# Inverting the gated delta rule's triangular matrices with block transposes on VectorE

## The chip, the cores and the metric

The kernel runs on one core of one Trainium2 chip. The metric is the device time of one execution in microseconds (us). Three executions of the kernel before took 2325.54, 2326.91 and 2327.57 us; their median, 2326.91 us, is the time before.

The engines are named as in the profile: PE (TensorE matmul), PEld (its weight loads), DVE (VectorE), ACT (ScalarE), POOL (GpSimd), SP (SyncE, which issues the weight DMAs).

## The reference, cut to what matters

Two layers, each with four token mixers and an MLP over 512 tokens of width 1024. The change concerns one mixer, the gated delta rule (4 heads, key and value width 128, chunks of 64 tokens):

```
h = rmsnorm(x, n_pre_mix); proj = h @ w_in
qkv = silu(causal_dwconv(gdn_qkv, conv_w))
beta = sigmoid(gdn_b); g = -exp(a_log) * softplus(gdn_a + dt_bias)
gc = cumsum(g over the chunk)                      # 8 chunks of 64 tokens
decay = exp(gc[c] - gc[s]) for c >= s
lower = strict lower part of (k * beta) @ k.T * decay       # 64 x 64 for each chunk and head
t_inv = inverse of (eye + lower)                   # triangular_solve
u = t_inv @ (v * beta); w = t_inv @ (k * beta * exp(gc))
attn = q @ k.T * decay
# over the chunks: v_new = u - w @ state; o = q*exp(gc) @ state + attn @ v_new
#                  state = state * exp(g_last) + k_dec.T @ v_new
```

The other parts (windowed attention, stick-breaking attention, retention, the output projections and the MLP) are as they were in both kernels.

## The kernel before, in words

All weights are float32. POOL splits every weight tile that SP loads into a high and a low part (lines 581 and 583), and a product of activations and weights is three fp32r matmuls (high by high, low by high, high by low) of 512 columns: line 1722, in `unit`. A unit is 256 rows of a weight matrix for 512 outputs: four output tiles by two row tiles by three matmuls. POOL may convert a further unit when PE has begun the next one (semaphore `w_used`).

The delta rule works on blocks of 128 tokens (two of the reference's chunks), numbered 0 to 3, with one 128 x 256 tile for the four heads' matrices: partition rows 0 to 63 and 64 to 127 hold two 64 x 64 matrices of each head. Blocks are inverted in pairs (b0 = 0, then b0 = 2), so there are two inverses in each layer and four in an execution. The two blocks of a pair, e = 0 and 1, are interleaved to cover each other's latencies.

The inverse is built by doubling. `g_T[e]` holds the running inverse in one orientation and `g_V[e]` its transpose; they are block diagonal. Level 0 is done on DVE (`first_level` writes `g_V`). Then, in the loop `for b0 in (0, 2)` of `tensor_layer`:

- T0: 64 x 64 matmuls with the identity turn `g_V` into `g_T`, by way of PSUM and an ACT copy (line 803).
- For level n = 1 to 5: Y = masked lower matrix times the even halves of T (PE), ACT copies Y out of PSUM (line 808), X = V times Y (PE), DVE subtracts X from the even halves of T (line 1409), V = T turned by matmuls with the identity (PE), ACT copies the turned halves to `g_V` (line 815), or at level 5 to `g_U` (line 818). A level n merges diagonal blocks of 2^n into blocks of 2^(n+1): after level 4 they are 32 wide, after level 5 64 wide.
- Level 6 joins the two chunks of a block (Y and X only).

`level_mask` on DVE (line 1245) makes the masked matrix of level n + 1 while level n runs. Between Y and X of levels 2, 3, 5 and 6 PE computes a quarter of a gate unit: one output tile with both row tiles, six matmuls (`QUARTERS`). In the trace all mixer matmuls have line 1867 (`MM1`), and one program matmul there counts as two instructions, so a Y or X or V pass over both blocks (16 matmuls) reads x32.

On DVE, `row_decays` (lines 1377 to 1380: a copy and two products) of the pair's blocks follow the X subtractions of levels 2 and 3. On ACT, the four value silus (`conv_silu(8)` to `(11)`, line 727) stand before the T0 copies. After the first inverse, blocks 0 and 1 run the recurrence, and prepare blocks 2 and 3 on the way. Block 3's score matmuls (`scores_gdn(3)`) and their masking on DVE (`scores_out(3)`, lines 1369 and 1371) come at the very end of that, ahead of the second inverse.

All orders are written out by hand: each engine runs its own program in order, and they meet at semaphores. `mixer_keys` lists the PSUM tiles of the mixers in order; they take four banks in turn, and a tile waits until the one four places before it has been freed.

## Time and profile before

| | us |
|---|---|
| median of three executions (lowest, highest) | 2326.91 (2325.54, 2327.57) |
| profiled execution, first to last instruction (span) | 2324.0 |
| PE busy in it | 2297.4 (99%) |
| DVE, ACT, POOL busy | 851.0, 751.4, 1282.2 |
| first inverse, from its T0 to the transposes behind it | 25.3 |

The span is the profiled execution's own time between its first and its last instruction; the median lies 2.9 us above it, which is what lies around the instructions. The granted TensorE clock was 0.997 over the span and 1.00 in the inverses, so 2.4 GHz. A busy PE in these rows is one with a matmul in flight: starts that lie further apart than the work needs do not show as idle time. So the places of the change are read from start to start.

### The profile page before, as it was taken

Reading aid. Unit: us, or ns where it says so; the run is one execution under the profiler, and the core shown is the slowest. Engines: PE = TensorE matmul, PEld = TensorE weight load, DVE = VectorE, ACT = ScalarE, POOL = GpSimd, SP = SyncE. Lnnn points to the kernel's source line nnn. Section 1 sums busy time; section 2 is a strip of 40 time slices with the busy share of each in tenths; the row PEclk is TensorE's granted clock in tenths of the full one; section 3 lists DMA queues with packets and bytes.
Section 4 is the critical chain, followed back from the end, with each engine's and each line's share of the span. In section 5 each row is a group of like instructions: output and inputs, shape, how many; then the busy total and the mean of one; then the engine's idle time right before and its main releaser. Section 6 shows DMA issues by size and latency. Waiting matters only on the chain.

```text
span 2324.0 us, 31844 instructions
## 1 busy us (share of the span) xinstructions
PE 2297.4 (99%) x13054; PEld 1870.2 (80%) x13054; DVE 851.0 (37%) x1350; ACT 751.4 (32%) x1505; POOL 1282.2 (55%) x732
## 2 busy tenths in 40 slices
PE   8999999999999999999999999999999999999998
PEld 7788877877877888888887888778778778888887
DVE  4543225334445521123355430254243445112233
ACT  5633226213035321122355341451230544112121
POOL 5513654554554566677655136546555445666874
PEclk9999999999999999999999999999999999999999
DMA  4311331322221243322222113213222213333331
GB/s 151 91 38 47 95 87 46 118 82 86 75 89 52 92 124 92 100 94 97 82 79 85 36 54 93 73 60 115 84 88 84 74 60 101 108 100 94 97 100 64
DMA packets 105904, 196.72 MB, mean 85 GB/s; under 512 B 8480, under 2 KB 18848, under 8 KB 105504
## 3 DMA queue, kind: packets, MB, share of 16 engines
q1 hardware_dynamic: 104608, 188.40, 26.8%
q10 hardware_dynamic: 1152, 6.29, 0.8%
q8 instruction: 104, 1.70, 0.3%
q14 instruction: 40, 0.33, 0.0%
HBM read 192.57 MB, written 2.10 MB: 84 GB/s over the span
## 4 chain that ended last, share of the span: by engine, by line
PE 96%; ACT 2%; DVE 2%; issue 1%; DMA 0%; DVEq 0%; ACTq 0%
PE big L1722 71%; PE mix L1722 9%; PE mix L1867 5%; PE big L2074 1%; PE mix L2042 1%; PE mix L2144 1%; PE mix L2053 1%; PE mix L1827 1%; PE mix L2272 0%; PE mix L2225 0%; PE mix L1781 0%; ACT o_hi L618 0%; PE mix L2209 0%; PE mix L2195 0%; PE mix L1999 0%
## 5 line engine op out<-in xcount | busy, mean ns | idle before, releaser
L583 POOL TENSOR_TENSOR ring_lo<-stage,ring_hi 128x1024 fp32r<-128x1024 f32 (+3 forms) x364 | 912.4, 2507 | 30.4
L581 POOL TENSOR_SCALAR ring_hi<-stage 128x1024 fp32r<-128x1024 f32 (+3 forms) x364 | 371.3, 1020 | 987.9 <-PE big L1722 906.6
L1722 PE MATMUL big<-h_hi,ring_hi 128*128 128x512 f32 (+1 forms) x1888 | 720.6, 382 | 3.0 <-DVE h_lo L1173 1.8
L1722 PE MATMUL big<-h_hi,ring_lo 128*128 128x512 f32 (+1 forms) x1888 | 709.3, 376 | 0.0
L1722 PE MATMUL big<-h_lo,ring_hi 128*128 128x512 f32 (+1 forms) x1888 | 709.2, 376 | 0.0
L1722 PEld LDWEIGHTS big<-h_hi,ring_hi 128*128 128x128 f32 x1888 | 355.4, 188 | 75.1 <-issue 8.6
L1722 PEld LDWEIGHTS big<-h_lo,ring_hi 128*128 128x128 f32 x1888 | 355.4, 188 | 65.7
L1722 PEld LDWEIGHTS big<-h_hi,ring_lo 128*128 128x128 f32 x1888 | 355.7, 188 | 62.9 <-issue 1.4
L1663 DVE TENSOR_TENSOR h_lo<-scr,h_hi 128x1024 fp32r<-128x1024 f32 x64 | 84.7, 1323 | 248.5 <-ACT h_hi L1091 248.5
L1722 PE MATMUL big<-ring_hi,h_hi 128*128 128x512 f32 x448 | 174.2, 390 | 0.0
L1722 PE MATMUL big<-ring_lo,h_hi 128*128 128x512 f32 x448 | 174.1, 390 | 0.0
L1722 PE MATMUL big<-ring_hi,h_lo 128*128 128x512 f32 x448 | 173.7, 389 | 0.0
L1091 ACT ACTIVATE h_hi<-scr 128x1024 fp32r<-128x1024 f32 x64 | 68.5, 1070 | 262.2 <-PE big L1722 260.2
L1674 DVE SCALAR_TENSOR_TENSOR scr<-big,scr 128x512 f32<-128x512 f32 x64 | 44.3, 692 | 254.5 <-ACT scr L1100 254.3
L1722 PE MATMUL mix<-ring_hi,h_hi 128*128 128x512 f32 x320 | 125.0, 391 | 0.0
L1722 PE MATMUL mix<-ring_hi,h_lo 128*128 128x512 f32 x320 | 124.6, 389 | 0.0
L1722 PE MATMUL mix<-ring_lo,h_hi 128*128 128x512 f32 x320 | 124.5, 389 | 0.0
L1100 ACT ACTIVATE scr<-big 128x512 f32<-128x512 f32 x64 | 38.3, 598 | 262.1 <-PE big L1722 261.3
L1722 PEld LDWEIGHTS big<-ring_hi,h_hi 128*128 128x128 f32 x448 | 84.1, 188 | 18.4 <-issue 0.7
L1722 PEld LDWEIGHTS big<-ring_hi,h_lo 128*128 128x128 f32 x448 | 84.1, 188 | 17.7
L1722 PEld LDWEIGHTS big<-ring_lo,h_hi 128*128 128x128 f32 x448 | 83.8, 188 | 18.0 <-POOL ring_lo L583 1.0
L1722 PE MATMUL big<-o_hi,ring_hi 128*128 128x512 f32 x224 | 90.2, 403 | 1.0 <-ACT scr L676 0.9
(304 smaller groups left out, 2758.0 us busy)
## 6 DMA issues: line engine op xcount, KB each, us to landing
stage<-in_w_in SPq DMA_DIRECT2D x168, 512.0 KB, 3.5
stage<-in_w_mlp_in SPq DMA_DIRECT2D x64, 512.0 KB, 3.7
stage<-in_w_mlp_out SPq DMA_DIRECT2D x64, 512.0 KB, 3.6
stage<-in_w_o SPq DMA_DIRECT2D x16, 512.0 KB, 3.6
stage<-in_w_br_a SPq DMA_DIRECT2D x8, 512.0 KB, 3.6
stage<-in_w_br_c SPq DMA_DIRECT2D x8, 512.0 KB, 3.6
stage<-in_w_br_d SPq DMA_DIRECT2D x8, 512.0 KB, 3.6
stage<-in_w_br_b SPq DMA_DIRECT2D x8, 512.0 KB, 3.6
```

What stands on the lines that cost most here:

```text
L581: nc.gpsimd.tensor_scalar(rH[jw][0:pp, r, 0:kk, 0:job.n], w, 1.0, 0.0, ALU.mult, ALU.add).then_inc(sem("w_hi"), 1)
L583: nc.gpsimd.tensor_tensor(rL[jw][0:pp, r, 0:kk, 0:job.n], w, f32(rH[jw][0:pp, r, 0:kk, 0:job.n]), ALU.subtract).then_inc(sem("w_ready"), 1)
L1091: A(hH[:, q:q + 2, :], fT[:, 2 * u:2 * u + 2, :], ACT.Copy).then_inc(sem("f_hi"), 1)
L1100: A(fT[:, 4 * g + i, :], ps[:, :], ACT.Relu).then_inc(sem("f_relu"), 1)
L1663: TT(hL[:, q:q + 2, :], fT[:, 2 * u:2 * u + 2, :], f32(hH[:, q:q + 2, :]), ALU.subtract).then_inc(sem("f_lo"), 1)
L1674: big_free(STT(fT[:, k, :], ps[:, :], 0.0, fT[:, k, :], ALU.max, ALU.mult), (f"up{g}", i))
L1722: ins_ = MM(o_, a_, r_, start=s0, stop=s1)
L1827: done(MM(ps[:, :], f32(ones_r[:, 0:1]).to_broadcast((P, P)), q_sq[:, i % 4, :], start=True, stop=True), ("l2", i))
L1867: return MM(o_, a_, b_, start=True, stop=True)
L2042: i = MM(c_bank[u][:, at:at + w], hv(cK, h)[:, j * P:(j + 1) * P], hv(cQ, h)[:, j * P:], start=opens, stop=True, skip_group_check=True)
L2053: MM(c_bank[u][:, :], rot_r[:, 2 * P:3 * P], part[:, u, :], start=False, stop=True, skip_group_check=True)
L2074: r = MM(c_out[e * DH:e * DH + DH, j * P:], cV[:, j, (2 * p + e) * DH:(2 * p + e + 1) * DH], c_A[:, u, at:at + S - j * P], start=j == 0, s ...
```

## The change

What it does:

- T0 and the V passes of levels 1 to 4 leave PE and ACT. As all diagonal blocks are at most 32 wide there, DVE's transpose, which turns every 32 x 32 block of a tile by itself, gives the same result: `first_inverse(b)` turns `g_V` into `g_T`, `inverse_turned(b, n)` turns `g_T` into `g_V`, each one instruction over 128 x 256 float32. The V pass of level 5 (blocks of 64) stays on PE and ACT.
- The gate unit that PE works on within an inverse is dealt in eighths (one output tile, one row tile: three matmuls) instead of quarters: after Y of all six levels and after X of levels 1 and 4.
- `row_decays` of the pair follow the levels 4 and 5 instead of 2 and 3. `natural_k_v(0)` waits for block 1's, as its output shares memory with what they read.
- The silus of value tiles 10 and 11 come after ACT's Y copies of levels 1 and 2 instead of before T0.
- `scores_gdn(3)` moves up on PE to stand behind `lower(3)`, ahead of `new(1)`. On DVE `scores_out(3)` is split: the product with the decays comes before `first_level(3)`, the masking (which overwrites what `o(1)` reads) waits for `o(1)`.
- The PSUM tiles of the mixers fall by 20 a layer, a multiple of the four banks, so the tiles behind keep their banks.

```diff
-QUARTERS = (2, 3, 5, 6)
+EIGHTHS = (("Y", 1), ("X", 1), ("Y", 2), ("Y", 3), ("Y", 4), ("X", 4), ("Y", 5), ("Y", 6))
...
     for b0 in (0, 2):
-        k += [("T0", b0), ("T0", b0 + 1)]
         for n in range(1, LEVELS):
-            for t in "YXV" if n < LEVELS - 1 else "YX":
+            for t in "YXV" if n == LEVELS - 2 else "YX":
                 k += [(t, b0 + e, n) for e in range(2)]
...
             k += [("R", b + 2), ("B", b + 2), ("LT", b + 2)] if ahead else []
+            k += [("att", 3)] if b == 1 else []
             k += [("new", b), ("o", b), ("dS", b)]
-        if b0 == 0:
-            k.append(("att", 3))
...
-            for i in range(8, 12):
-                conv_silu(i)
+            conv_silu(8)
+            conv_silu(9)
             for b0 in (0, 2):
-                for e in range(2):
-                    ps = mix_wait(act, ("T0", b0 + e))
-                    act.wait_ge(*upto("a_attd", b0 + e + 1))
-                    mix_free(A(g_T[e], ps[:, 0:GH * HB], ACT.Copy), ("T0", b0 + e))
...
+                    if b0 == 0 and n in (1, 2):
+                        conv_silu(9 + n)
-                    for e in range(2) if n < LEVELS - 1 else ():
+                    for e in range(2) if n == LEVELS - 2 else ():
                         ps = mix_wait(act, ("V", b0 + e, n))
...
+            def first_inverse(b):
+                dve.wait_ge(*upto("a_attd", b + 1))
+                mix_freed(dve, ("LT", b))
+                V.transpose(g_T[b % 2], g_V[b % 2]).then_inc(sem("a_T0"), 1)
+            def inverse_turned(b, n):
+                mix_freed(dve, ("X", b, n))
+                V.transpose(g_V[b % 2], g_T[b % 2]).then_inc(sem("a_V"), 1)
...
                         mix_free(i, key)
-                    if n in (2, 3):
-                        row_decays(b0 + n - 2)
+                    for e in range(2) if n < LEVELS - 2 else ():
+                        inverse_turned(b0 + e, n)
+                    if n in (4, 5):
+                        row_decays(b0 + n - 4)
...
                         lower(b + 2)
+                        if b == 1:
+                            scores_out(3)
                         first_level(b + 2)
+                        if b == 1:
+                            first_inverse(3)
+                    if b == 1:
+                        scores_masked(3)
                     ps = mix_wait(dve, ("dS", b))
...
+            def eighth(t, n):
+                if (t, n) in EIGHTHS:
+                    i = EIGHTHS.index((t, n))
+                    unit(*(fills.pop(0) if i == 7 else fills[0]), (i // 2,), rows_of=range(i % 2, i % 2 + 1))
...
-                        mix_freed(pe, ("T0", b0 + e) if n == 1 else ("X", b0 + e, n - 1))
+                        if n == 1:
+                            pe.wait_ge(*upto("a_T0", b0 + e + 1))
+                        else:
+                            mix_freed(pe, ("X", b0 + e, n - 1))
...
-                        if n > 1:
+                        if n == LEVELS - 1:
                             mix_freed(pe, ("V", b0 + e, n - 1))
+                        elif n > 1:
+                            pe.wait_ge(*upto("a_V", (LEVELS - 3) * b0 + 2 * (n - 2) + e + 1))
...
+                    if b == 1:
+                        scores_gdn(3)
                     mix_freed(pe, ("ks", b))
                     mix_freed(pe, ("X", b, LEVELS - 1))
```

PE's row in the first inverse, before: T0, then Y, X and V of level 1, Y of level 2, a quarter of the gate unit, and X of level 2. `big` is a gate's bank, `mix` a mixer's, `g_uc` is `g_V`, `consts` the identity, `scr` all else of the mixer.

```order
L1867 MATMUL mix<-consts,g_uc 64x64 x16
L1867 MATMUL mix<-scr 64x32 x16
L1867 MATMUL mix<-scr,g_uc 64x32 x16
L1867 MATMUL mix<-consts,scr 64x32 x16
L1867 MATMUL mix<-scr 64x32 x16
L1722 MATMUL big<-h_hi,ring_hi 128x512
L1722 MATMUL big<-h_hi,ring_lo 128x512
L1722 MATMUL big<-h_lo,ring_hi 128x512
L1722 MATMUL big<-h_hi,ring_hi 128x512
L1722 MATMUL big<-h_hi,ring_lo 128x512
L1722 MATMUL big<-h_lo,ring_hi 128x512
L1867 MATMUL mix<-scr,g_uc 64x32 x16
```

The change, from the same place: Y of level 1, an eighth, X, an eighth, Y of level 2, an eighth.

```order
L1895 MATMUL mix<-scr 64x32 x16
L1744 MATMUL big<-h_hi,ring_hi 128x512
L1744 MATMUL big<-h_hi,ring_lo 128x512
L1744 MATMUL big<-h_lo,ring_hi 128x512
L1895 MATMUL mix<-scr,g_uc 64x32 x16
L1744 MATMUL big<-h_hi,ring_hi 128x512
L1744 MATMUL big<-h_hi,ring_lo 128x512
L1744 MATMUL big<-h_lo,ring_hi 128x512
L1895 MATMUL mix<-scr 64x32 x16
L1744 MATMUL big<-h_hi,ring_hi 128x512
L1744 MATMUL big<-h_hi,ring_lo 128x512
L1744 MATMUL big<-h_lo,ring_hi 128x512
```

The two passes with `consts` are gone, and every run of `big` rows is three long.

DVE's row over levels 1 to 3 before: masks (line 1245), subtractions of X (line 1409), the first row decays (1377 to 1380).

```order
L1245 TENSOR_TENSOR scr<-scr,consts 128x256 x2
L1409 TENSOR_TENSOR scr<-scr,mix 128x64x2 x2
L1245 TENSOR_TENSOR scr<-scr,consts 128x256 x2
L1409 TENSOR_TENSOR scr<-scr,mix 128x32x4 x2
L1377 COPY st<-scr 128x4
L1379 TENSOR_TENSOR scr<-scr 128x4x128
L1380 TENSOR_TENSOR scr<-scr 128x512
L1245 TENSOR_TENSOR scr<-scr,consts 128x256 x2
L1409 TENSOR_TENSOR scr<-scr,mix 128x16x8 x2
```

The change, levels 1 to 3: masks (now line 1238), subtractions (now line 1424), and the transposes of both blocks (line 1368).

```order
L1238 TENSOR_TENSOR scr<-scr,consts 128x256 x2
L1424 TENSOR_TENSOR scr<-scr,mix 128x64x2 x2
L1368 STREAM_TRANSPOSE g_uc<-scr 128x256 x2
L1238 TENSOR_TENSOR scr<-scr,consts 128x256 x2
L1424 TENSOR_TENSOR scr<-scr,mix 128x32x4 x2
L1368 STREAM_TRANSPOSE g_uc<-scr 128x256 x2
L1238 TENSOR_TENSOR scr<-scr,consts 128x256 x2
L1424 TENSOR_TENSOR scr<-scr,mix 128x16x8 x2
L1368 STREAM_TRANSPOSE g_uc<-scr 128x256 x2
```

Two transposes stand behind each pair of subtractions, so the masks of the level after next stand behind the transposes; the row decays have left these levels.

DVE's row at the end of block 1 before: `scores_out(2)`, `lower(3)`, `first_level(3)`, the four state updates of block 1 (line 1433).

```order
L1369 TENSOR_TENSOR mix<-mix,scr 128x512
L1371 TENSOR_TENSOR scr<-mix,consts 128x512
L1349 TENSOR_TENSOR mix<-mix,scr 128x256
L1351 TENSOR_TENSOR scr<-mix,scr 64x256
L1353 TENSOR_TENSOR scr<-mix,consts 128x256
L1360 TENSOR_TENSOR mix<-mix,consts 128x256
L1364 TENSOR_TENSOR g_uc<-scr,mix 128x256
L1433 SCALAR_TENSOR_TENSOR scr<-scr,st,mix 128x128 x4
```

The change: `lower(3)`, the first half of `scores_out(3)` (line 1373), `first_level(3)`, `first_inverse(3)` (1363), the masking of block 3's scores (1383), the state updates (1457), and the first masks of the second inverse.

```order
L1342 TENSOR_TENSOR mix<-mix,scr 128x256
L1344 TENSOR_TENSOR scr<-mix,scr 64x256
L1346 TENSOR_TENSOR scr<-mix,consts 128x256
L1373 TENSOR_TENSOR mix<-mix,scr 128x512
L1353 TENSOR_TENSOR mix<-mix,consts 128x256
L1357 TENSOR_TENSOR g_uc<-scr,mix 128x256
L1363 STREAM_TRANSPOSE scr<-g_uc 128x256
L1383 TENSOR_TENSOR scr<-mix,consts 128x512
L1457 SCALAR_TENSOR_TENSOR scr<-scr,st,mix 128x128 x4
L1238 TENSOR_TENSOR scr<-scr,consts 128x256 x2
```

Block 3's masking now stands ahead of block 1's state updates, with a wait for PE's `o(1)`.

## Rows read from the trace of the kernel before

**Rows 1.** The page, parts 1 and 4: engines; share of the span by line.

```profile
PE 2297.4 (99%) x13054; PEld 1870.2 (80%) x13054; DVE 851.0 (37%) x1350; ACT 751.4 (32%) x1505; POOL 1282.2 (55%) x732
...
PE big L1722 71%; PE mix L1722 9%; PE mix L1867 5%; PE big L2074 1%; PE mix L2042 1%; PE mix L2144 1%; PE mix L2053 1%; PE mix L1827 1%; PE mix L2272 0%; PE mix L2225 0%; PE mix L1781 0%; ACT o_hi L618 0%; PE mix L2209 0%; PE mix L2195 0%; PE mix L1999 0%
```

**Rows 2.** Busy time by engine in the first inverse (columns in the first row).

```profile
core 0: us, PE busy (x) PEld busy (x) DVE busy (x) ACT busy (x) POOL busy (x), PEclk, DMA share, GB/s
114.60:139.95 25.35, 25.08 (x570) 22.06 (x569) 10.41 (x26) 9.56 (x28) 4.67 (x3) 1.00 0.15 44
```

**Rows 3.** Timeline of PE, first inverse: start us, us, engine line op tiles xcount [idle].

```profile
114.61 1.15 PE L1867 MATMUL mix<-consts,g_uc 64*64 64x64 f32 x32
115.96 1.12 PE L1867 MATMUL mix<-scr 64*64 64x32 f32 x32 [0.21 <-issue]
117.08 1.12 PE L1867 MATMUL mix<-scr,g_uc 64*64 64x32 f32 x32
118.21 1.12 PE L1867 MATMUL mix<-consts,scr 64*64 64x32 f32 x32
119.13 1.13 PE L1867 MATMUL mix<-scr 64*64 64x32 f32 x32
120.19 0.50 PE L1722 MATMUL big<-h_hi,ring_hi 128*128 128x512 f32 x1
120.53 0.40 PE L1722 MATMUL big<-h_hi,ring_lo 128*128 128x512 f32 x1
...
121.46 0.39 PE L1722 MATMUL big<-h_lo,ring_hi 128*128 128x512 f32 x1
121.78 1.12 PE L1867 MATMUL mix<-scr,g_uc 64*64 64x32 f32 x32
...
130.75 1.12 PE L1867 MATMUL mix<-consts,scr 64*64 64x32 f32 x32
131.67 1.13 PE L1867 MATMUL mix<-scr 64*64 64x32 f32 x32
...
139.95 0.66 PE L1893 MATMUL mix<-consts,scr 128*128 128x128 f32 x4
```

**Rows 4.** The same view, inverses two and three.

```profile
167.03 1.15 PE L1867 MATMUL mix<-consts,g_uc 64*64 64x64 f32 x32
168.25 1.17 PE L1867 MATMUL mix<-scr 64*64 64x32 f32 x32
...
192.31 0.66 PE L1893 MATMUL mix<-consts,scr 128*128 128x128 f32 x4
...
1266.43 1.15 PE L1867 MATMUL mix<-consts,g_uc 64*64 64x64 f32 x32
...
1291.81 0.66 PE L1893 MATMUL mix<-consts,scr 128*128 128x128 f32 x4
```

**Rows 5.** Timeline of DVE: last value convolution, level 1, behind level 2.

```profile
114.18 0.75 DVE L1293 SCALAR_TENSOR_TENSOR scr<-mix,lw,scr 128x509 f32<-128x509 f32 x1
...
117.77 0.29 DVE L1409 TENSOR_TENSOR scr<-scr,mix 128x128 f32<-128x128 f32 x1 [0.22 <-PE mix L1867]
118.24 0.29 DVE L1409 TENSOR_TENSOR scr<-scr,mix 128x128 f32<-128x128 f32 x1 [0.18 <-PE mix L1867]
...
123.15 1.22 DVE L1377 COPY st<-scr 128x4 f32<-128x4 f32 x1
```

**Rows 6.** Timeline of POOL, same stretch.

```profile
121.99 2.35 POOL L583 TENSOR_TENSOR ring_lo<-stage,ring_hi 128x1024 fp32r<-128x1024 f32 x1
```

**Rows 7.** Two lines of DVE: instructions, ns min/median/max.

```profile
L1245 DVE TENSOR_TENSOR scr<-scr,consts x32: 409/426/428, 116.7 to 1333.9; 128x256 f32<-128x256 f32 x32
...
L1440 DVE TENSOR_TENSOR scr<-scr x16: 680/693/2924, 224.2 to 1716.0; 128x512 f32<-128x512 f32 x16
```

**Rows 8.** Timelines of PE and of DVE, end of block 1 in layer 1.

```profile
165.15 1.95 PE L1867 MATMUL mix<-scr 128*128 128x128 f32 x16
...
166.25 1.12 DVE L1433 SCALAR_TENSOR_TENSOR scr<-scr,st,mix 128x128 f32<-128x128 f32 x4 [4.11 <-PE mix L1867]
```

More of the change, by code:

```diff
@@ L1396, in vector_layer @@
                 first_level(b)
+                first_inverse(b)
             for i in range(8, 12):
@@ L1919, in tensor_layer @@
             for b0 in (0, 2):
-                for e in range(2):
-                    mix_freed(pe, ("LT", b0 + e))
-                    ps = tile_of(("T0", b0 + e))
-                    for h in range(GH):
-                        for rows in HALVES:
-                            i = MM1(ps[rows, h * HB:(h + 1) * HB], blocks(g_V[e])[rows, h, :], ident[rows, rows])
-                    done(i, ("T0", b0 + e))
                 for n in range(1, LEVELS):
@@ L1943, in tensor_layer @@
                         done(i, key)
-                    if n in QUARTERS:
-                        t = QUARTERS.index(n)
-                        unit(*(fills.pop(0) if t == NT - 1 else fills[0]), (t,))
+                    eighth("Y", n)
                     for e in range(2):
@@ L1960, in tensor_layer @@
                         done(i, key)
-                    for e in range(2) if n < LEVELS - 1 else ():
+                    eighth("X", n)
+                    for e in range(2) if n == LEVELS - 2 else ():
                         key = ("V", b0 + e, n)
@@ L1966, in tensor_layer @@
                             for rows in HALVES:
[L1967 to L1969 removed]
+                                i = MM1(ps[rows, h * HB:(h + 1) * HB], blocks(g_T[e])[rows, h, :], ident[rows, rows])
                         done(i, key)
```

48 lines of the change are left out of this document (23 added, 25 removed), and 12 rows, old and new, of the table PER_LAYER.

## The prediction

> **What bounds the kernel now.** I read the page first. PE is busy for 99% of the span and the chain that ended last is nearly all PE, 71% in gate and projection units and 5% in the mixer's matmuls of line 1867 [rows 1]. A microsecond taken from PE's own row is therefore a microsecond of the kernel, as long as nothing else is late in its place. Then I read the windows of an inverse: in 25.35 us PE is busy 25.08, DVE 10.41, ACT 9.56, POOL 4.67, with the clock at 1.00, the 2.4 GHz level [rows 2]. DVE has about 15 us to spare in it. Then the timeline of PE, from start to start, since a busy PE hides short waits [rows 3]. The reader is to see there that a pass over both blocks is followed after 1.12 us if the next pass needs its result by way of ACT or DVE, and after 0.92 us if it does not (V to Y: 118.21 to 119.13, and at level 4 130.75 to 131.67). So 0.92 is what PE needs, and 0.20 is a wait.
>
> **Removed from PE.** T0 took 115.96 - 114.61 = 1.35 us (with 0.21 idle until ACT had copied), in the second inverse 168.25 - 167.03 = 1.22 [rows 3, 4]. Each of the four V passes of levels 1 to 4 took 0.92, together 3.68. In their place PE now goes from X to Y of the next level; X to V was 1.13 (117.08 to 118.21), waiting for DVE's subtraction, and X to Y waits for the same subtraction, so that step stays. Removed: 5.03 us in the first inverse of a layer, 4.90 in the second.
>
> **Added on PE: smaller helpings.** From Y to X with a quarter between is 121.78 - 119.13 = 2.65 us, without one 1.12. A quarter costs 1.53 for six products whose starts are (121.46 - 120.53) / 4 = 0.23 apart, so 1.38 of work. Going over to 512-column products and back costs the rest, 0.15, net of the wait that it covers [rows 3]. The products are as many as before (8 x 3 = 4 x 6), but there are four more changes over: 4 x 0.15 = 0.6 us an inverse. An eighth costs 0.69 + 0.15 = 0.84, and from Y to X it is then 1.12 + 0.84 = 1.96.
>
> **Added on DVE: the transposes.** No row of before shows one; ten to an inverse, counting those that replace T0. Bounds from DVE's products: 128 columns take 0.29 [rows 5], 256 take 0.43 [rows 7], so 0.15 fixed and 0.14 for 128 columns. A transpose of 256 columns would take 0.29 at twice that pace, 0.43 at the same, 0.71 at half and 1.27 at a quarter of it. I take 0.43, the row of the same shape. The Trainium skill ("Vector Engine (DVE) Microarchitecture Reference", section 3.8) says that the transposing front end sustains one element per cycle and lane; no run here shows that yet, and an estimate by it is the same 0.43 or so.
>
> Whether it is hidden follows from DVE's row. Count from the start of X of level n. The subtractions start at 0.69 and 1.16 and end at 1.45 [rows 3, 5]. Two transposes T bring it to 1.45 + 2T, two masks at 0.43 to 2.31 + 2T. The next X starts 1.13 + 1.96 = 3.09 later and DVE's next subtraction is due 0.69 behind that, at 3.78. So T may be 0.73 before PE waits; with 0.43 there are 0.6 us left. Behind level 1, and from X of level 4 to X of level 5, an eighth more makes the period 3.93. There T may be 1.15 behind level 1, and behind level 4, where two row decays take the place of the masks (0.16 and 2 x 0.6, an estimate from 1.2 us for two products of 512 columns back to back, 0.69 each less their overlap), 0.9. In the first inverse `first_inverse(1)` also pushes the value convolutions back by 0.4 us. The last of them (line 1293) ended at 114.18 + 0.75 = 114.93, 0.3 into the inverse [rows 5]; its bank is first needed by X of block 1, 2.4 us into it.
>
> POOL is the second thing to hold against DVE. The copy of line 1377 took 1.22 us for four columns; it ended at 124.37, and POOL's product ran from 121.99 to 124.34 [rows 5, 6]. Products of two SBUF operands range from 0.69 to 2.92 in the same way (line 1440) [rows 7]. The Trainium skill ("SBUF — State Buffer", section "Who interferes with whom") says that one of the two holds a shared port pair for its whole instruction while the other stands still, that a copy and a DVE instruction with two SBUF inputs are subject to it, and that one with a single SBUF input outside the two-port modes is not; by that rule, the trace agrees for the copy (1.22 us), and the transposes go free. In the change the new unit begins with the first eighth, 1.12 - 0.06 = 1.06 us after the inverse's first Y (119.13 to 120.19 in before), and POOL's product ends 4.15 after that (120.19 to 124.34), at 5.21. The masks for level 3 have two SBUF inputs; they end at 5.21 + 0.86 = 6.07. X of level 2 starts at 1.96 + 3.93 = 5.89 and the subtraction is due at 6.58. It holds by 0.5 us: 0 is added.
>
> **Moved at no cost.** The silus of tiles 10 and 11 go where ACT has just lost its T0 and V copies; their cover is ACT's idle time (25.35 - 9.56). They are needed only behind the inverse, and if that cover were gone PE would wait at the value transposes for one silu. The row decays leave the levels in which the transposes now stand; blocks 0 and 1's are needed when the inverse is over, 5 us and 3 us later. Block 3's score matmuls are the same work in another place. What they change: the first Y of the second inverse needs the bank that `scores_masked(3)` frees. Before, state matmuls starting at 165.15 let DVE go on at 166.25, 1.10 later [rows 8], their 0.88 of work and 0.22 behind it. In the change they start 0.88 later, `o(1)` is seen by DVE at 165.15 + 0.88 + 0.22 = 166.25, a masking of 0.69 (the median of line 1440, same shape) and 0.15 to PE make 167.09, against 167.03 where T0 began. I add 0.06. The state updates behind it are not needed until the inverse is over; they start with the state matmuls' result at 166.25 + 0.88 = 167.13, end 1.12 later, and two masks bring DVE to 169.1, where the first subtraction is due at 167.09 + 1.96 + 0.69 = 169.74.
>
> **The sum.** First inverse: 5.03 - 0.6 = 4.43 saved, of 25.34 (114.61 to 139.95). Second: 4.90 - 0.6 - 0.06 = 4.24. Layer 2 repeats it (1266.43 to 1291.81 is 25.38) [rows 4]. Together 2 x 8.67 = 17.3 us. The profiled execution would go from 2324.0 to 2306.7; the median of the runs lies 2.9 above the span, so from 2326.9 to 2309.6. Weights are no bound: POOL is busy 55% [rows 1], and all stages behind only start earlier.
>
> **Rivals.**
> - POOL blocks the transposes too. For: they have one SBUF input, as the copy has that was blocked. Against: at most one pair falls into POOL's work, that of level 1. It would start at 5.21, and with the masks behind it end at 5.21 + 1.72 = 6.93, 0.35 late. Four times that is 1.4 us: 2311.0. In a layer's first inverse `first_inverse(1)` could wait too, at most for one product of POOL, 2.35; the convolutions would then end 0.3 + 2.35 = 2.65 into the inverse, 0.3 late. That makes 2 x 0.3 more, 2311.6.
> - The transposes are slow, but not so slow as to lose. Between T = 0.73 and 1.4 each inverse gives back 4(T - 0.73) for levels 2 and 3, 2(T - 0.9) and 2(T - 1.15) once T passes these. At 1.0: 1.28 an inverse, 2314.7. At 1.27, four times the columns' pace: 3.1 an inverse, 2322.1. For: four-byte data in an operation that no row shows. Against: the DVE rows over f32 that POOL does not hold up keep to 0.14 us for 128 columns.
> - Slower than before: DVE becomes the bound in levels 1 to 4. The place is the pair of transposes between subtraction and masks, the price 8 us for each us of T in an inverse beyond the points above, and it decides from 8T - 7.02 = 4.33, so T = 1.42. At T = 1.7 it would give back 6.5 an inverse and end at 2336. For: a transposer that fills and then drains for each of eight blocks without overlap, plus stalls behind POOL. Against: that is over three times the row of the same shape.
> - The gaps are worth less than they look: PE's weight loads, no longer covered by V passes, or changes over at 0.3 instead of 0.15. Four more changes and eight in all: 0.6 to 1.2 an inverse, 2312 to 2314.
>
> **How the numbers follow.** The forecast with T up to 0.73 and all covers holding: 0.65. POOL's blocking 0.1, slow transposes with a gain 0.11, dearer changes over 0.09, slower 0.05. The likeliest time is 2309.6. Nothing here can save more than PE's 5.0 an inverse without the changes over, 20 in all: 2307. The upper end takes in the dearer changes, blocking and T to 1.15: 2319. A difference of 0.2%, 4.7 us, is about what a measurement of this kernel can tell from none. Faster by more needs a time below 2322.3: 0.88. Within 0.2%: T from 1.27 to 1.5 or several small losses together, 0.07. Slower: 0.05.
>
> **What would show it right or wrong.** Right: transposes of 0.4 to 0.5 us; Y to X 1.96 with an eighth between; X to Y 1.13 at levels 2 and 3; from the first Y to the key transposes 20.9 us; the second inverse starting within 0.1 us of the state matmuls' end. Wrong: subtractions that start later than 0.69 after their X, which is the mark of DVE behind; a transpose as long as POOL's product beside it; PE waiting for `a_V`.

## The result

The changed kernel takes 2310.39 us, the median of 4 runs (2306.62 to 2310.90); the kernel before took 2326.22 in the same comparison (4 runs, 2325.43 to 2327.57). The ratio of this comparison is 0.9922 (95% interval 0.9906 to 0.9938); the two medians alone give 0.9932, inside that interval, and 15.8 us less. The profiled execution took 2309.96 us with a span of 2308.2, against a span of 2324.0 before, so the two traces differ by the same 15.8 us. The forecast was 2309.6 us, 17.3 less than the kernel before.

The page first, with the lines that answer to [rows 1]. In the kernel now the helper of the units is L1744, that of the mixer's matmuls L1895, the key transposes are L1921.

```profile
PE 2282.2 (99%) x12414; PEld 1848.9 (80%) x12414; DVE 862.5 (37%) x1390; ACT 739.5 (32%) x1465; POOL 1281.5 (56%) x732
...
PE big L1744 72%; PE mix L1744 10%; PE mix L1895 4%; PE big L2097 1%; PE mix L2065 1%; PE mix L2167 1%; PE mix L2076 1%; PE mix L1855 1%; PE mix L2295 1%; PE mix L2248 0%; PE mix L1809 0%; ACT o_hi L616 0%; PE mix L2232 0%; PE mix L2218 0%; PE mix L2024 0%
```

PE has 640 matmul instructions fewer and is as full as before. DVE has 40 instructions more, ACT 40 fewer. PE is still the bound, so the time is to be found in its own row. The first inverse by engine, the answer to [rows 2], and two stretches of 20 us that the change does not touch (columns in the first row):

```profile
core 0: us, PE busy (x) PEld busy (x) DVE busy (x) ACT busy (x) POOL busy (x), PEclk, DMA share, GB/s
113.55:134.29 20.74, 20.72 (x409) 16.85 (x409) 12.89 (x35) 6.83 (x19) 4.71 (x3) 1.00 0.18 53
720.00:740.00 20.00, 20.00 (x67) 12.72 (x66) 8.88 (x13) 12.09 (x14) 6.76 (x5) 0.83 0.17 52
1870.00:1890.00 20.00, 20.00 (x70) 12.92 (x66) 6.82 (x10) 9.24 (x9) 8.11 (x5) 0.74 0.17 48
```

The inverse went from 25.34 to 20.73 us, with 0.02 idle and the clock at 1.00. The timeline of PE in it, which answers to [rows 3] (start us, us, engine line op tiles xcount):

```profile
113.56 1.12 PE L1895 MATMUL mix<-scr 64*64 64x32 f32 x32
114.61 0.50 PE L1744 MATMUL big<-h_hi,ring_hi 128*128 128x512 f32 x1
...
115.51 1.12 PE L1895 MATMUL mix<-scr,g_uc 64*64 64x32 f32 x32
...
117.45 1.12 PE L1895 MATMUL mix<-scr 64*64 64x32 f32 x32
...
119.40 1.12 PE L1895 MATMUL mix<-scr,g_uc 64*64 64x32 f32 x32
120.49 1.12 PE L1895 MATMUL mix<-scr 64*64 64x32 f32 x32
...
134.29 0.44 PE L1921 MATMUL mix<-consts,scr 128*128 128x128 f32 x2
```

From a Y to the X behind it, with an eighth between, it is 117.45 to 119.40, 1.95 us (1.96 was forecast); from X to the next Y without an eighth 119.40 to 120.49, 1.09 (1.13). No row has an idle time. The four inverses, from the first Y to the key transposes, take 20.73, 20.75, 20.73 and 20.74 us, against 25.34, 25.28, 25.38 and 25.34 from the start of T0 before [rows 3, 4]: 4.61 + 4.53 + 4.65 + 4.60 = 18.4 us.

The span shortened by 15.8 only. Laid one on the other, the traces are apart by 1.05 us where the first inverse begins. Near the start, in the first row below, the kernel before had a clock of 0.83 and the changed one 1.00, but that does not explain the 1.05: another execution of the changed kernel, also with 1.00 there, begins its first inverse at 114.45 and not at 113.56, and the kernel before began at 114.61. So most of it differs from one execution to the next and is not the change's. The traces are 10.18 apart behind the second inverse, but 8.10 where the third begins; 17.35 behind the fourth, but 15.8 at the end. So 2.08 and 1.55 us were lost in stages that the change leaves alone: 18.4 + 1.05 - 2.08 - 1.55 = 15.8. The windows of the kernel before there (columns as above):

```profile
10.00:20.00 10.00, 8.18 (x48) 7.78 (x47) 5.72 (x24) 9.16 (x29) 9.75 (x7) 0.83 0.92 347
730.00:750.00 20.00, 20.00 (x74) 13.55 (x74) 10.49 (x13) 12.18 (x14) 7.72 (x5) 0.91 0.15 53
1880.00:1900.00 20.00, 20.00 (x67) 12.82 (x66) 8.88 (x13) 14.15 (x17) 6.47 (x5) 0.83 0.18 53
```

PE is busy for all of the two later windows and the clock is 0.91 and 0.83; in the changed kernel, in the same work, 0.83 and 0.74. A mean of 0.83 over 20 us is 3.4 us of work not done, so before 1.8 + 3.4 = 5.2 and now 3.4 + 5.2 = 8.6. These dips were there before and each costs 1.6 to 1.8 us more now. A second trace of the changed kernel has both as deep, so they are not of one execution alone; its two fastest executions (2306.62 and 2307.77 us) have a mean clock of 0.997 over the span, the others 0.995 or 0.996.

PE is busy there, but with what? In both stages it goes through seven products (14 instructions) whose operands have only three rows, and in every trace the clock falls in the middle of them or right behind them. The changed kernel, then the kernel before (start us, us), and the windows of the changed kernel:

```profile
723.18 6.19 PE L2295 MATMUL mix<-scr,consts 3*128 3x512 f32 x14
...
733.31 4.89 PE L2272 MATMUL mix<-scr,consts 3*128 3x512 f32 x14
```

```profile
723.18:726.60 3.42, 3.42 (x12) 1.05 (x12) 1.93 (x4) 1.75 (x3) 0.00 (x0) 1.00 0.04 17
726.60:729.30 2.70, 2.70 (x4) 0.65 (x2) 2.44 (x5) 1.37 (x3) 0.00 (x0) 0.51 0.00 0
```

In the changed kernel the clock falls at 726.6, within the run of these products, and in the kernel before at 738.7, behind its end at 738.2. How deep a dip comes out goes with where in that run the clock falls. In the 28 dips of all the traces here, a fall up to 2.5 us behind the run's start costs 5.1 us, one at 2.9 to 4.3 us costs 3.4, and one at 4.5 us or later 1.7. Here the fall came at 3.4 and 2.2 us, in the kernel before at 5.4 and 3.7. Why it comes earlier in one kernel than in another no run here shows.

The transposes themselves, both lines of DVE (instructions, ns min/median/max, first and last start):

```profile
L1368 DVE STREAM_TRANSPOSE g_uc<-scr x32: 401/420/439, 116.9 to 1319.8; 128x256 f32<-128x256 f32 x32
...
L1363 DVE STREAM_TRANSPOSE scr<-g_uc x8: 433/445/446, 100.2 to 1301.7; 128x256 f32<-128x256 f32 x8
```

They take 0.42 us; 0.43 was taken. In a pair they start 0.34 to 0.36 apart, so a pair is 0.76. Now the place where POOL's work and DVE's meet. DVE, level 1 to level 2 of the first inverse:

```profile
116.89 0.77 DVE L1368 STREAM_TRANSPOSE g_uc<-scr 128x256 f32<-128x256 f32 x2
118.16 1.26 DVE L1238 TENSOR_TENSOR scr<-scr,consts 128x256 f32<-128x256 f32 x2 [0.51 <-PE mix L1895]
120.10 0.29 DVE L1424 TENSOR_TENSOR scr<-scr,mix 128x128 f32<-128x128 f32 x1 [0.68 <-PE mix L1895]
```

POOL, the product that lies beside it:

```profile
116.43 2.37 POOL L581 TENSOR_TENSOR ring_lo<-stage,ring_hi 128x1024 fp32r<-128x1024 f32 x1
```

The pair of transposes ran from 116.89 to 117.66, inside POOL's product, in its usual 0.77 us. The two masks behind it took 1.26 instead of 0.72 and ended at 119.42, that is 0.62 after the product's end at 118.80. The subtraction had been due at 120.10 and started then, 0.70 after its X at 119.40. So POOL holds up the masks and not the transposes, and PE does not wait.

The second inverse, PE and then DVE, the answer to [rows 8]:

```profile
160.40 2.11 PE L1895 MATMUL mix<-scr 128*128 128x128 f32 x40
...
163.33 1.12 PE L1895 MATMUL mix<-scr,g_uc 64*64 64x32 f32 x32
```

```profile
160.60 0.69 DVE L1383 TENSOR_TENSOR scr<-mix,consts 128x512 f32<-128x512 f32 x1 [3.27 <-PE mix L2024]
161.50 1.12 DVE L1457 SCALAR_TENSOR_TENSOR scr<-scr,st,mix 128x128 f32<-128x128 f32 x4 [0.20 <-PE mix L1895]
162.54 0.76 DVE L1238 TENSOR_TENSOR scr<-scr,consts 128x256 f32<-128x256 f32 x2
```

The group at 160.40 holds eight state matmuls and the first Y. The X at 163.33 is 1.95 behind that Y, which therefore began at 161.38, 0.98 after the state matmuls: 0.88 of work and 0.10. DVE had masked block 3's scores from 160.60 on.

### The profile page after: what moved, and what is told of

It reads as the page before. It is cut to its first block, busy times and chain, and to the rows that moved or that the text cites. A ratio compares the mean times of both kernels' runs of the same rounds, so it can differ in the third digit from the quotient of the medians.

```text
span 2308.2 us, 30524 instructions
## 1 busy us (share of the span) xinstructions
PE 2282.2 (99%) x12414; PEld 1848.9 (80%) x12414; DVE 862.5 (37%) x1390; ACT 739.5 (32%) x1465; POOL 1281.5 (56%) x732
## 4 chain that ended last, share of the span: by engine, by line
PE 95%; ACT 2%; DVE 2%; issue 1%; DMA 0%; DVEq 0%; ACTq 0%
PE big L1744 72%; PE mix L1744 10%; PE mix L1895 4%; PE big L2097 1%; PE mix L2065 1%; PE mix L2167 1%; PE mix L2076 1%; PE mix L1855 1%; PE mix L2295 1%; PE mix L2248 0%; PE mix L1809 0%; ACT o_hi L616 0%; PE mix L2232 0%; PE mix L2218 0%; PE mix L2024 0%
## 5 line engine op out<-in xcount | busy, mean ns | idle before, releaser
L1744 PE MATMUL big<-h_hi,ring_hi 128*128 128x512 f32 (+1 forms) x1888 | 721.5, 382 | 2.9 <-DVE h_lo L1166 1.7
L1744 PE MATMUL big<-h_lo,ring_hi 128*128 128x512 f32 (+1 forms) x1888 | 708.6, 375 | 0.0
L1744 PE MATMUL big<-h_hi,ring_lo 128*128 128x512 f32 (+1 forms) x1888 | 708.5, 375 | 0.0
L1744 PEld LDWEIGHTS big<-h_hi,ring_hi 128*128 128x128 f32 x1888 | 354.7, 188 | 74.9 <-issue 8.9
L1744 PEld LDWEIGHTS big<-h_lo,ring_hi 128*128 128x128 f32 x1888 | 354.7, 188 | 66.0
L1744 PEld LDWEIGHTS big<-h_hi,ring_lo 128*128 128x128 f32 x1888 | 355.0, 188 | 62.0 <-issue 1.4
L1744 PE MATMUL big<-ring_hi,h_hi 128*128 128x512 f32 x448 | 174.2, 390 | 0.0
L1744 PE MATMUL big<-ring_lo,h_hi 128*128 128x512 f32 x448 | 174.1, 390 | 0.0
L1744 PE MATMUL big<-ring_hi,h_lo 128*128 128x512 f32 x448 | 173.7, 389 | 0.0
L1744 PE MATMUL mix<-ring_hi,h_hi 128*128 128x512 f32 x320 | 125.0, 391 | 0.0
L1744 PE MATMUL mix<-ring_hi,h_lo 128*128 128x512 f32 x320 | 124.6, 389 | 0.0
L1744 PE MATMUL mix<-ring_lo,h_hi 128*128 128x512 f32 x320 | 124.5, 389 | 0.0
L1744 PEld LDWEIGHTS big<-ring_hi,h_hi 128*128 128x128 f32 x448 | 84.1, 188 | 18.1 <-issue 0.7
L1744 PEld LDWEIGHTS big<-ring_lo,h_hi 128*128 128x128 f32 x448 | 83.8, 188 | 18.2 <-POOL ring_lo L581 1.0
L1744 PEld LDWEIGHTS big<-ring_hi,h_lo 128*128 128x128 f32 x448 | 84.1, 188 | 17.6
L1744 PE MATMUL big<-o_hi,ring_hi 128*128 128x512 f32 x224 | 90.4, 403 | 1.0 <-ACT scr L674 0.9
```

Source lines behind the costliest of these rows:

```text
L1744: ins_ = MM(o_, a_, r_, start=s0, stop=s1)
```

## The experiments

Medians are of the runs of one comparison; each ratio is against the kernel before on the same chip. "Inverses" are the four lengths as above.

**Is DVE's slack what the sum said?** A spare transpose ahead of each level transpose, then two:

```diff
             def inverse_turned(b, n):
...
+                for j in range(1):          # second kernel: range(2)
+                    V.transpose(scr[:, gslot(16 + j) + GH * HB:gslot(16 + j) + 2 * GH * HB], g_T[b % 2]).then_inc(sem("a_spare"), 1)
```

> The changed kernel with one spare transpose (128 x 256, into unused memory) ahead of each of the 16 level transposes of a layer. It tests the price that the prediction gave to slow transposes. By its formula, T goes from 0.42 to 0.84 and each inverse (first Y to key transposes, 20.73 us in the changed kernel) grows by 4 x (0.84 - 0.73) = 0.44 us. By the rows of the changed kernel DVE has 0.95 us to spare between two subtractions at levels 2 and 3 and a further pair of transposes costs 0.69: nothing, 20.7 to 20.8 us. Rival, that DVE already sets the pace: 0.7 us for each of levels 1 to 4, 23.5 us.

> The changed kernel with two spare transposes ahead of each level transpose, so DVE does three where one is wanted. By the prediction's formula T = 1.26: 4 x 0.53 + 2 x 0.36 + 2 x 0.11 = 3.1 us more an inverse, 23.8 us, and 12 us more in all. By the rows of the changed kernel (0.95 us to spare at levels 2 and 3, 1.2 at level 4, 1.4 us added): 0.5 twice and 0.3, so 22 us an inverse and 5 us in all. If DVE's time were hidden altogether: 20.7 us.

Doubled: 2310.05 us in one run, span 2308.2, the same as the changed kernel; the first and third inverse take 20.74. The formula wanted 0.44 an inverse. Tripled: 2312.36 (4 runs, 2309.16 to 2313.69), ratio 0.9942 (0.9928 to 0.9957); the inverses are 0.29, 0.37, 0.26 and 0.27 longer, 1.2 us in all, where the formula gave about 12. DVE of the tripled kernel shows why (L1372 spare, L1373 wanted, L1238 masks, L1429 subtractions):

```profile
120.51 0.76 DVE L1372 STREAM_TRANSPOSE scr<-scr 128x256 f32<-128x256 f32 x2
121.20 0.40 DVE L1373 STREAM_TRANSPOSE g_uc<-scr 128x256 f32<-128x256 f32 x1
121.53 0.73 DVE L1372 STREAM_TRANSPOSE scr<-scr 128x256 f32<-128x256 f32 x2
122.18 0.41 DVE L1373 STREAM_TRANSPOSE g_uc<-scr 128x256 f32<-128x256 f32 x1
122.50 0.72 DVE L1238 TENSOR_TENSOR scr<-scr,consts 128x256 f32<-128x256 f32 x2
123.14 0.57 DVE L1429 TENSOR_TENSOR scr<-scr,mix 128x128 f32<-128x128 f32 x2
123.63 0.76 DVE L1372 STREAM_TRANSPOSE scr<-scr 128x256 f32<-128x256 f32 x2
```

DVE has no gap left here, and one level goes round in 123.63 - 120.51 = 3.12 us, against PE's 3.04 from X to X. Six transposes fit into 122.50 - 120.51 = 1.99, 0.33 each; two masks take 0.64. The durations of single rows, 0.43, were added up in the forecast, although rows that follow each other overlap. That holds for the masks (0.64 for two, not 0.86) and the subtractions (0.49 for two) as well: with 0.33 for each added transpose, T = 1.08, the formula would still want 1.8 us an inverse. The mechanism, DVE as the next bound, is right and the price of it was about ten times too high.

**What does each moved part do?** First the transposes without the moves: the kernel before, with the VectorE transposes, but with quarters after Y at levels 2, 3, 5 and 6, row decays at levels 2 and 3, all silus ahead and block 3's scores behind block 1.

```diff
-        k += [("T0", b0), ("T0", b0 + 1)]
-            for t in "YXV" if n < LEVELS - 1 else "YX":
+            for t in "YXV" if n == LEVELS - 2 else "YX":
...
+                    for e in range(2) if n < LEVELS - 2 else ():
+                        inverse_turned(b0 + e, n)
```

> The kernel before with the transposes on DVE and nothing else: quarters, row decays after levels 2 and 3, all four silus ahead of the first inverse, block 3's scores at the end of block 1. If the transposes bring the gain and the rest is trimming, it keeps most of the 15.8 us. My theory: the other parts are cover for the transposes. Quarters save 0.5 us an inverse against eighths, but the decays make DVE 1.4 us late, the silus hold the first Y copy by 0.8 us in a layer's first inverse, and block 3's scores hold first_inverse(3), 1.6 us in the second. Sum against the changed kernel: +8 us, so 7 to 9 us faster than before, about 2318. Rival: PE is bound anyway and all but the transposes is worth nothing, 2308 to 2312.

2329.70 us (10 runs, 2321.72 to 2346.00), ratio 1.0020 (0.9997 to 1.0043): nothing is gained, though T0 and V are gone. The profiled execution was the fastest of the ten, with a span of 2319.9. Its inverses take 21.90, 24.37, 23.42 and 24.38 us, 7.3 less in all than before. The slower executions have a lower mean clock, from 0.994 at 2321.72 to 0.979 at 2346.00 us. PE at the start of the second inverse:

```profile
165.51 0.66 PE L1888 MATMUL mix<-scr 64*64 64x32 f32 x16 [1.47 <-issue]
...
169.19 0.63 PE L1737 MATMUL big<-h_hi,ring_lo 128*128 128x512 f32 x1
```

```profile
163.00:167.00 4.00, 2.53 (x66) 2.25 (x66) 3.40 (x9) 0.56 (x2) 0.00 (x0) 1.00 0.00 0
167.00:171.00 4.00, 4.00 (x48) 3.31 (x44) 1.70 (x5) 0.56 (x2) 1.36 (x2) 0.61 0.00 0
```

PE sat idle for 1.47 us, then went on with thin 64x64 products. From 167 to 171 the mean clock is 0.61, most of it at the lower level, 0.50 (1.2 GHz), and a 512-column product that takes 0.40 elsewhere takes 0.63. Each of the four inverses has two idle times: 0.70 in the first of a layer, waiting for ACT's first copies behind the silus, 1.47 in the second, and 1.07 in all four, ahead of Y of level 5, for a subtraction. Together they are 8.6 us, near the 8 that were expected. Behind three of the eight the clock fell: behind the one above and behind two of 1.07, in the third and the fourth inverse (to 0.72 over 1279 to 1285 and over 1330 to 1336). Behind the other five, one of 1.47 among them, it stayed at 1.00. So in this execution falls come on top of the expected 8 us. The lower clocks of the slower executions suggest more of them; no trace shows one of those.

Then one part at a time was put back into the changed kernel. Quarters again:

```diff
-                if (t, n) in EIGHTHS:
...
+                if t == "Y" and n in (2, 3, 5, 6):
+                    i = (2, 3, 5, 6).index(n)
+                    unit(*(fills.pop(0) if i == 3 else fills[0]), (i,))
```

> The changed kernel with the gate unit dealt in quarters after Y of levels 2, 3, 5 and 6, all else as changed. Four changes over to 512-column products fewer, at 0.14 us each. If nothing is late at levels 1 and 4, where PE then goes straight on, each inverse is 0.5 us shorter: 20.2 us, and 2 us in all. Rival: the eighths are needed as cover, the subtractions of levels 1 and 4 start over 0.7 us after their X and the inverse is 20.7 us or longer.

2307.28 us (4 runs, 2307.04 to 2308.04), ratio 0.9923 (0.9908 to 0.9938), span 2305.7. Inverses 20.09, 20.12, 20.37 and 22.46. The first two are 0.63 to 0.64 shorter than with eighths, four changes over at 0.16 each (0.15 was taken). In the third, Y of level 5 takes 1.40 instead of 1.12, a wait of 0.28; the fourth has an idle time of 0.70 in the middle of a pass, with the clock down behind it, from 1317 to 1321 at 0.59:

```profile
1316.83 0.54 PE L1895 MATMUL mix<-scr 64*64 64x32 f32 x13 [0.70 <-issue]
...
1317.63 0.54 PE L1744 MATMUL big<-h_hi,ring_lo 128*128 128x512 f32 x1
```

The four sum to 83.0 us as in the changed kernel (82.95), so the 2.5 us of span are not from them: its dips in the two untouched stages cost 1.7 and 3.4 us, as in the kernel before, which is 3.4 less, and its first inverse begins 0.75 later. The ratio cannot tell it from the changed kernel.

Row decays at levels 2 and 3 again:

```diff
-                    if n in (4, 5):
-                        row_decays(b0 + n - 4)
+                    if n in (2, 3):
+                        row_decays(b0 + n - 2)
```

> The changed kernel with the row decays after levels 2 and 3 again. They take DVE 1.33 us, and it has 0.95 us to spare between two subtractions there: 0.4 us late at each of two levels, 21.5 us an inverse (20.73 with them at 4 and 5) and 3 us in all. Rival, that the move was free either way: 20.7 us.

2310.93 us (4 runs, 2308.37 to 2312.10), ratio 0.9926 (0.9912 to 0.9939). Each inverse is 0.22 to 0.25 longer, 0.9 us in all. The direction is as expected, the size a third: PE is idle for 0.20 once in each inverse, where DVE was expected to be late at two levels. The silus first again:

```diff
-            conv_silu(8)
-            conv_silu(9)
+            for i in range(8, 12):
+                conv_silu(i)
```

> The changed kernel with all four value silus ahead of the first inverse. The last convolution ends 0.85 us after the first Y starts; a silu of 0.63 and the Y copy of 0.28 behind it let X start about 2.0 us after Y, where the eighth lets it start at 1.95. So 0 to 0.1 us in each layer's first inverse, 20.7 to 20.8, nothing in the second. Rival: the whole silu shows, 0.6 us.

2310.85 us in one run, all inverses 20.73 or 20.74: no effect. The parts do not simply add, though. In the kernel with the transposes alone, where no eighth follows Y of level 1 and none X of level 4, the silus leave PE idle for 0.70 and the decays for 1.07; so it seems to be the eighths that make the other two moves cheap or free.

Block 3's scores behind block 1 again, and with them on DVE `first_inverse(3)`, which writes over their decays and so has to follow them:

```diff
-                        if b == 1:
-                            scores_out(3)
...
-                        if b == 1:
-                            first_inverse(3)
...
+                if b0 == 0:
+                    scores_out(3)
+                    first_inverse(3)
...
-                    if b == 1:
-                        scores_gdn(3)
...
+                if b0 == 0:
+                    scores_gdn(3)
```

> The changed kernel with block 3's scores at the end of block 1 again, on PE and DVE; first_inverse(3) then follows them, as it writes over their decays. After the score matmuls DVE needs 0.22 + 0.69 + 0.69 + 0.45 and PE 0.15 to see it, 2.2 us, and block 3's first Y is due 0.5 us after them: 1.6 us lost in the second inverse of each layer, 3.3 in all. Rival: DVE's order does not matter, since a whole inverse of cover is there: 0.

2327.69 us (10 runs, 2322.38 to 2341.81), ratio 1.0009 (0.9991 to 1.0027), so 17 us slower than the changed kernel where 3.3 were expected. This one move undoes everything. PE at the start of the second and of the fourth inverse, and the windows there (columns as above):

```profile
164.18 0.66 PE L1890 MATMUL mix<-scr 64*64 64x32 f32 x16 [1.47 <-issue]
...
1308.92 0.66 PE L1890 MATMUL mix<-scr 64*64 64x32 f32 x16 [1.47 <-issue]
```

```profile
164.00:185.00 21.00, 20.81 (x397) 16.97 (x398) 12.29 (x35) 4.55 (x15) 3.42 (x2) 1.00 0.09 27
...
1310.00:1312.00 2.00, 2.00 (x36) 1.57 (x34) 0.33 (x2) 0.00 (x0) 1.75 (x2) 0.71 0.04 8
1312.00:1344.00 32.00, 32.00 (x349) 26.21 (x349) 11.40 (x32) 4.38 (x14) 1.66 (x1) 0.50 0.06 18
```

Both times PE is idle for 1.47 us. Its row names no releaser, but block 3's Y needs the matrix that `first_inverse(3)` turns: in layer 1 this row of DVE ends at 164.07, and PE goes on at 164.18.

```profile
163.64 0.43 DVE L1364 STREAM_TRANSPOSE scr<-g_uc 128x256 f32<-128x256 f32 x1
```

In layer 1 the clock stays at 1.00 and the inverse takes 22.4 us, 1.6 more than 20.74, as expected. In layer 2 the clock falls between 1310 and 1312 and stays at 0.50 for all of the 32 us of the last row: the fourth inverse, from its first Y at 1306.79, takes 35.7 us. The same wait costs 1.6 us once and 14.9 another time. The ten executions are 19 us apart, and the clock goes with it: its mean over the span is 0.991 at 2322.38 us and 0.982 at 2341.81, and 0.009 of the span is 21 us.

**Is it the idle time?** If it is, block 3's scores may stay late as long as PE has other work there. Two eighths are put ahead of the first Y of the second inverse:

```diff
+                if b0 == 2:
+                    eighth("Y", 1)
+                    eighth("X", 1)
...
-                    eighth("Y", n)
+                    if b0 == 0 or n > 1:
+                        eighth("Y", n)
```

> Block 3's scores at the end of block 1, as in the run before it with late scores (median 2327.7, PE idle for 1.47 us ahead of the second inverse, granted clock at 0.50 for the whole of the fourth inverse), but the second inverse's first two eighths stand ahead of its first Y instead of after Y and X of level 1, so that PE has 1.6 us of dense products where it was idle. My theory: the idle time costs its 1.5 us and also lets the clock fall in the thin matmuls behind it; with it filled the clock stays at 1.00 in all four inverses and the time is within 2 us of the changed kernel's 2310.4. Rival: late scores are dear for another reason (the clock falls by chance, or by the thin matmuls alone), and the median stays above 2318 with clock rows of 0.5 in an inverse.

2337.64 us (4 runs, 2336.99 to 2338.91), ratio 1.0042 (1.0027 to 1.0056): the slowest of all. The expectation failed, but the run is no test of the theory, since the edit made another wait. DVE, POOL and PE there:

```profile
164.42 0.43 DVE L1364 STREAM_TRANSPOSE scr<-g_uc 128x256 f32<-128x256 f32 x1
164.91 2.49 DVE L1239 TENSOR_TENSOR scr<-scr,consts 128x256 f32<-128x256 f32 x2
167.32 0.47 DVE L1422 TENSOR_TENSOR scr<-scr,mix 128x128 f32<-128x128 f32 x2
```

```profile
164.43 2.35 POOL L582 TENSOR_TENSOR ring_lo<-stage,ring_hi 128x1024 fp32r<-128x1024 f32 x1
```

```profile
167.69 1.12 PE L1890 MATMUL mix<-scr 64*64 64x32 f32 x32 [0.97 <-DVE scr L1422]
```

The eighths freed a weight buffer earlier than in the kernel with late scores alone, POOL's product now began at 164.43 and not at 166.55, just ahead of the masks of level 2; they took 2.49 instead of 0.72, the subtraction came late, and PE was idle for 0.97 us between two thin passes. The windows behind it:

```profile
169.00:171.00 2.00, 2.00 (x27) 1.44 (x26) 0.38 (x2) 0.13 (x1) 0.00 (x0) 0.61 0.45 170
171.00:195.00 24.00, 24.00 (x284) 19.89 (x283) 8.66 (x25) 3.83 (x12) 0.00 (x0) 0.50 0.01 1
```

The second inverse took 31.1 us and the fourth 32.4, though two of their eighths now stand ahead of them; the first and third, untouched, 20.73.

**How few helpings will do?** A whole unit after Y of level 6; then 12 + 12 products after Y of levels 3 and 6; then 9 + 6 + 9 after Y of levels 2, 4 and 6. In all three both row decays stand behind level 5. The cut shows the kernel with three helpings; that with two has {3: 4, 6: 4}, and that with one calls `unit` once for the whole unit.

```diff
-                    if n in (4, 5):
-                        row_decays(b0 + n - 4)
+                    if n == 5:
+                        row_decays(b0)
+                        row_decays(b0 + 1)
...
+            helpings = {2: 3, 4: 2, 6: 3}
...
+                first = sum(helpings[m] for m in helpings if m < n)
+                for i in range(first, first + helpings.get(n, 0)) if t == "Y" else ():
```

> The changed kernel with the whole gate unit (24 products) in one helping after Y of level 6, and both row decays after level 5. Seven changes over fewer at 0.14 us: 1.0 us an inverse. PE then goes through levels 1 to 5 without cover; a period of 2.21 us, against DVE's 1.37 + 0.69 + 0.72 = 2.78 us from X, with the next subtraction due at 2.91: 0.1 us to spare. POOL's conversion falls behind all masks. So 19.9 us an inverse with some tenths for level 1, 3 us faster than the changed kernel: 2307. Rival: DVE and its own bubbles are late at each of levels 1 to 4 by 0.2 us or more, and nothing is gained: 20.7 us.

> The changed kernel with the gate unit in two helpings of 12 products, after Y of level 3 and after Y of level 6, and both row decays after level 5. One helping gave 19.43 us an inverse; one change over more costs 0.14, so 19.57, 1.2 less than the changed kernel: 2305.8 if the clock holds. Longest thin stretch of PE 5 us (one helping: 13). If a long stretch of thin matmuls lets the clock fall (one helping had 0.87 and 0.79 in the third inverse), the two helpings show 1.00 in all inverses and a narrower spread. Rival: the falls are chance, and the two kernels spread alike.

> The same with three helpings (9, 6 and 9 products, after Y of levels 2, 4 and 6) and both row decays after level 5. 19.43 + 2 x 0.14 = 19.7 us an inverse, 2306.4 with the clock at 1.00 throughout. By the theory that DVE has time to spare only if no POOL conversion falls on the masks, the conversion now stands beside the masks of level 4, and an inverse may take up to 0.3 more. Rival: as in e10, the falls are chance.

| kernel | median us, n (range) | ratio to before | inverses us |
|---|---|---|---|
| one helping | 2305.70, 5 (2303.11 to 2312.46) | 0.9910 (0.9895 to 0.9925) | 19.43, 19.43, 22.76, 19.42 |
| two | 2304.96, 4 (2303.18 to 2309.32) | 0.9903 (0.9887 to 0.9919) | third 23.29, others 19.7 to 20.0 |
| three | 2305.35, 5 (2305.19 to 2308.84) | 0.9906 (0.9891 to 0.9921) | 20.04, 20.49, 20.01, 19.85 |

Seven changes over fewer shorten an undisturbed inverse by 20.74 - 19.43 = 1.31, 0.19 each. With one and with two helpings one inverse in the profile has a fallen clock (0.59 from 1266 to 1274, behind an idle of 0.15; 0.57 from 1271 to 1279, behind one of 0.64). With three none has, although its second inverse has an idle time of 0.39, and the four sum to 80.4 against 82.95. Its span is 2303.4, 4.8 below the changed kernel's; 2.6 of that are the inverses. Of the two untouched stages' dips, which are smaller here (compare 0.83 and 0.74 above), come 3.4, and the first inverse begins 1.0 later:

```profile
720.00:740.00 20.00, 20.00 (x75) 13.47 (x74) 10.73 (x13) 12.10 (x14) 7.40 (x5) 0.91 0.17 52
1860.00:1880.00 20.00, 20.00 (x68) 12.52 (x67) 8.97 (x13) 13.60 (x17) 6.74 (x5) 0.83 0.17 54
```

All three beat both kernels by their medians. Against the changed kernel the intervals overlap, so the order among them is not settled.

**The changed kernel once more**, unedited, on the chip of the kernels with two and three helpings:

> The changed kernel once more, on the chip of these runs, to set the helpings against it. 2310 as before (2306.6 to 2310.9), clock 1.00 in all four inverses, 20.7 us each. If its spread is over 5 us here, differences of 3 us between kernels say nothing.

2311.25 us (5 runs, 2307.77 to 2311.33), ratio 0.9924 (0.9911 to 0.9938); clock 1.00 in all four inverses, which take 20.72 to 20.74 us.

## Why the prediction was right

The time, 2310.39 against 2309.6, is right and for the reason given: passes of PE that another engine could do were taken from PE's own row, and nothing came late in their place. Against the 17.3 us that it promised, 15.8 were measured; the two times lie as close as 0.8 us also because the kernel before was 0.7 faster in this comparison. Step by step:

- **Removed from PE and changes over.** 4.43 and 4.24 us an inverse were forecast, 4.61 and 4.53 measured (4.65 and 4.60 in layer 2). A change over costs 0.16 by the kernel with quarters; X to Y is 0.04 shorter than taken.
- **Transposes.** 0.43 taken, 0.42 measured.
- **Hidden behind PE.** Right, with far more room than the sum gave. The slack formula added whole durations; measured, a transpose behind another costs 0.33. It promised a loss from T = 0.73 on. Twice the transposes cost nothing and three times cost 0.3 an inverse. The rival "slow transposes" was priced by this formula and would probably have been cheaper too, though no run here has a slower transpose.
- **POOL.** The product was to end 5.21 after the first Y, at 118.77; it ended at 118.80. The masks were to end at 6.07, at 119.63; they ended at 119.42. The subtraction was not late. The rival in which POOL blocks the transposes is excluded by the pair that ran inside POOL's product in 0.77 us, and by `first_inverse(1)`, which took 0.45 us from 105.09 on inside the product from 104.25 to 106.66.
- **Second inverse.** 0.06 late was taken. Y started 0.98 behind the start of the state matmuls, 0.88 of them work, so a wait of 0.1 at most is left, within what was named.
- **Silus.** Nothing, as forecast and as their own run shows.
- **Row decays and block 3's scores** stood under "moved at no cost". They cost nothing, but the list did not ask what is lost without them. Left where they were, the decays give back 0.9 us and the scores, with the transpose behind them, 17. That second number is the whole gain. It is the one step in which the forecast's reasoning was thin: the 1.47 us of idle PE that the scores' old place would have left, with DVE's transpose of block 3 behind them, was not worked out, nor what the clock may make of it.
- **Stages behind "only start earlier".** They also got slower: their clock dips ate 2.6 us net of what the start gave (+1.05, -2.08, -1.55). The inverses gave 1.1 us more than forecast, and this took it back and 1.5 more. The 1.05 at the start is mostly chance, and so part of the agreement is luck.

**What stays open.** The traces have nine falls of the clock to 0.50 inside an inverse, each 0.1 to 2.4 us behind an idle time of PE of 0.15 to 1.47 us in or ahead of the thin products, and none in the inverses of the changed kernel, which have no such idle time (traces of two executions). But an idle time is not enough. Behind 14 others the clock stayed at 1.00: 0.21 and 0.22 in the kernel before (the first in [rows 3]), 0.2 in each inverse of the kernel with early decays, five of 0.70 to 1.47 with the transposes alone, the 1.47 of layer 1 with late scores, 0.20 with two helpings, and this one with three:

```profile
178.14 0.79 PE L1898 MATMUL mix<-scr 64*64 64x64 f32 x10 [0.39 <-issue]
```

Nor is it needed: in the two untouched stages the clock falls in or behind products of three rows with no idle time at all. The run that was to show that filling the wait keeps the clock made a new one. So what decides whether the clock falls is open. Why PE is idle for 0.64 and 0.70 in the middle of a pass, where no engine is named as the releaser, is open as well, and may be a sign of the fall rather than its cause.

## What to carry to other kernels

Passes that only re-order data can leave a full TensorE for VectorE blocks at their full worth, if each idle time that their going uncovers is filled in the same change: the transposes alone gained nothing here. Price a wait of TensorE among thin matmuls not by its length alone; 1.47 us cost 1.6 once and 14.9 us another time. To find out how much room an engine has, take its back-to-back rows from start to start, not the sum of their durations.

## What the runs showed of the hardware

- A VectorE transpose of 128x256 f32 in blocks takes 0.42 us (0.40 to 0.45), and 0.33 from start to start when one follows another. A POOL product of two SBUF operands does not hold it up; a VectorE product of two SBUF operands in the same place goes from 0.72 for two to 1.26, and to 2.49 in the run with late scores and early eighths.
- TensorE's granted clock fell from 1.00 to 0.50 inside nine inverses, 0.1 to 2.4 us behind an idle time of 0.15 to 1.47 us. In three of them it stayed there for 31 to 34 us, while 64x64 products ran with helpings of 512 columns between them: 31.1 to 35.7 us for an inverse of 20.7. Behind 14 idle times of 0.19 to 1.47 us in such products it did not fall.
- It also fell with TensorE never idle, in or right behind seven products of three rows (at 726.6 in a run of them from 723.18 to 729.37). In the 28 such runs of products that were traced, the later in the run the clock fell, the less the dip cost: 5.1, 3.4 or 1.7 us.
- Going over from 64x64 tiles to 512-column products and back costs 0.16 to 0.19 us.
- These dips, in stages that no edit touched, differ from one kernel to another by 1.7 us each, a third of what a measurement of this kernel can tell.
